# A two-layer retention / convolution / mixture-of-experts trunk: the router's product on two column tiles, slot and block numbers from the position, and its one-hot tables shared out over Pool, ScalarE and VectorE

## The chip, the cores and the metric

One core of one Trainium2 chip runs the whole forward pass. The metric is the device time of one execution in microseconds (us), lower is better. Engines are called as in the profile: PE is TensorE (PEld its weight loads), DVE VectorE, ACT ScalarE, POOL GpSimd, SP SyncE, which here only issues transfers.

## The reference, cut to what matters

512 tokens of width 1024 pass through two layers. Layer 0 mixes tokens by retention, layer 1 by a convolution module; behind each mixer stands a mixture of experts with 4 groups of 8 experts, all in f32. What the change touches is the router ahead of the experts:

```python
    lg = (xt @ w_rg + b_rg).astype(jnp.float32)
    pg = jax.nn.softmax(lg, axis=-1)
    g_idx = jnp.argmax(lg, axis=-1).astype(jnp.int32)
    gate_g = jnp.take_along_axis(pg, g_idx[:, None], axis=-1)
    le = (xt @ w_re + b_re).astype(jnp.float32).reshape(N, MOE_GROUPS, MOE_EXPERTS_PER_GROUP)
    le_sel = jnp.take_along_axis(le, g_idx[:, None, None], axis=1)[:, 0]
    top_v, top_i = lax.top_k(le_sel, MOE_TOPK)
    pe = jax.nn.softmax(top_v, axis=-1)
    wts = (gate_g * pe).reshape(-1)
    eid = (g_idx[:, None] * MOE_EXPERTS_PER_GROUP + top_i.astype(jnp.int32)).reshape(-1)
    ...
        return (jax.nn.silu(xblk @ w_gate[e]) * (xblk @ w_up[e])) @ w_down[e]
    ...
    out = jax.ops.segment_sum(yb * buf_w[:, None].astype(yb.dtype), buf_tok, num_segments=N + 1)[:N]
```

The assignments (two for each token) are sorted by expert and cut into blocks that belong to one expert each; which slot of which block a token lands in is free, as long as its result comes back with its weight.

## The kernel before, in words

**Layers.** In each layer the mixer comes first (weight tiles split in two parts by ACT and POOL, products on PE), then x is turned (transposed) by PE (turn_x, L640), then the router runs (route: PE L712, DVE L1022), then the experts (PE L795, DVE L1136, ACT L496, POOL L445 to L456).

**Experts.** The 1024 assignments are laid out in blocks of 32 rows; each block belongs to one expert, an expert has at least one block, and there are 47 blocks in each layer here (the 94 executions of the lines of a block are two layers of 47). Block by block PE multiplies by gate and up (L770), by down (L790), picks the rows of the next block from the normed x by one-hot products (pick_rows, L700), turns them (L709), and sends the result of the block before to its tokens (put_rows, L753). The weights of an expert are three transfers of 2 MB on SP's queue (L361 to L381); nine places in SBUF hold three experts. The first three experts are loaded ahead of the router or under it; the transfer for expert 3 and every later one waits until the blocks of the expert that holds the place are done (semaphores gu_half, gu_mm, y_mm).

**The router, in the order in which each engine meets it.** The order is written by hand, and each engine runs its own list in order.

- PE: eight products of the turned x with the router's weights (L716), all into the same 36 partitions of bank 0; it waits for DVE's copy of the result, turns it in four pieces (L721) and then runs six matmuls whose result nobody reads (stay_awake, L651). It waits for the one-hot table of experts, counts with nine products (L728, L730), runs four more unread matmuls, picks the rows of block 0 (L700), turns them (L709), waits for spread_ready and multiplies the table of slots with the table of blocks (L742), which gives for each block the token and the weight of each row. Then the first expert begins (L770).
- ACT: copies the even pieces of the turned x (L487), then squares x and takes roots (L467, L468), scales x by the reciprocal root (L493), and takes two exponentials (L498, L500). Then it waits for the first block.
- DVE: copies the odd pieces (L961), then takes the reciprocal of the roots (L966), and only after it copies the product (L1024); then some forty small instructions in a chain (Link.done, L88, waits for each before the next is issued) up to pos (L1090), the row of every assignment among all blocks. know_rows (L988) makes from pos the one-hot rows of block 0. Five small steps (L1093 to L1097) make the slot in the block and the number of the block from rank and base. Then come block_hot (L1100, 576 columns a partition), slot_hot_r (L1103, 1024 columns), the copy of the picked rows (stage, L1020), and three copies of block_hot scaled by the three rows of coef (L1107, L1110, L1112), with turned_block (L1008) in between. After them it makes the rows of block 1 and reads the product L742.
- POOL: has nothing in the router. It waits for idx_ready and for the token numbers (L445, L446), whose transfer SP issues after idx_mm (L358).
- SP: the transfer into place 8 waits for the end of the router's product (L354), the loop over the later experts for cum_ready and idx_mm (L356, L357).

The three scaled tables are written over by the later experts' work; slot_hot_r lies where sine and cosine lay before.

Of the kernel before, what the change touches and what calls it, by code (L numbers as in the profile page):

```python
# [21 lines left out]
ALU = mybir.AluOpType  # L22
ACT = mybir.ActivationFunctionType
# [6 lines left out]
P = 128  # L30
# [27 lines left out]
C_EYE, NCONST = 630, 662  # L58
# [34 lines left out]
def program(nc, x_in, pos_in, const_in, decay_in, par_in, w_qk, w_v, w_g, w_out, w_pw1, w_pw2, b_pw2,  # L93
            w_router, b_router, w_gu0, w_gu1, w_down, g_final, tok_in, out):
    with ExitStack() as ctx:
# [104 lines left out]
        logitsT = area_c[0:NG + NE, route_at:route_at + S]  # L200
# [8 lines left out]
        ranki, blki = room[:, 1816:1824].bitcast(I32), room[:, 1824:1832].bitcast(I32)  # L209
        count, blocks, upto = room[:, 1832:1864].bitcast(I32), room[:, 1864:1896], room[:, 1896:1928]  # L210
# [47 lines left out]
        def both(name):  # L258
            return sems(name, NL)
# [4 lines left out]
        tok_loaded, slot_known, tok_hot, y_split, y_rounded, first_mm, second_mm, added = (  # L264
            both(n) for n in ("tok_loaded", "slot_known", "tok_hot", "y_split", "y_rounded", "first_mm", "second_mm", "added"))
# [154 lines left out]
        def _(pool):  # L420
# [12 lines left out]
            for l in range(NL):  # L433
                if l == 1:
                    for n in range(pw1_tiles + 2 * TILES):
# [8 lines left out]
                        split_lo(ret_tiles + n, n % NWT, n // TILES % 4, tile_column(False, n % TILES))  # L444
                pool.wait_ge(idx_ready[l], 1)  # L445
# [14 lines left out]
        def _(act):  # L460
# [35 lines left out]
            def expert_blocks(l):  # L496
# [3 lines left out]
                nc.scalar.activation(expert_exp, expert_exp, ACT.Exp).then_inc(exp_ready[l], 1)  # L500
                act.wait_ge(cum_ready[l], 1)
# [128 lines left out]
        def _(pe):  # L630
# [81 lines left out]
            def route(l):  # L712

                for k in range(KT):
                    pe.wait_ge(hT_odd if k % 2 else hT_even, 4 * l + k // 2 + 1)
                    last = nc.tensor.matmul(ps[0:NG + NE, 0, :], wr[:, l, k, :], hT[:, k, :],  # L716
                                            start=(k == 0), stop=(k == KT - 1))
                last.then_inc(logitT_mm[l], 1)
                pe.wait_ge(logitT_ready[l], 1)
                for i in range(NT):  # L720
                    last = nc.tensor.transpose(ps[:, 1, i * 64:i * 64 + NG + NE], logitsT[:, i * P:(i + 1) * P],  # L721
                                               ident[0:NG + NE, 0:NG + NE])
# [17 lines left out]
                pe.wait_ge(spread_ready[l], 1)  # L740
                for j in range(8):
# [199 lines left out]
        def _(dve):  # L941
# [80 lines left out]
            def route(l, gain):  # L1022
                dve.wait_ge(logitT_mm[l], 1)
                V.tensor_copy(logitsT, ps[0:NG + NE, 0, :]).then_inc(logitT_ready[l], 1)  # L1024
# [17 lines left out]
                for i in range(NT):  # L1042
# [48 lines left out]
                                       op0=ALU.mult, op1=ALU.add).then_inc(hot_step[l], 1)  # L1091
                know_rows(l, 0)
                link.done(V.tensor_copy(ranki[:, :], rank[:, :]))  # L1093
                link.done(V.tensor_single_scalar(blki[:, :], ranki[:, :], 5, ALU.arith_shift_right))
                link.done(V.tensor_single_scalar(ranki[:, :], ranki[:, :], BLK - 1, ALU.bitwise_and))
                link.done(V.tensor_copy(rank[:, :], ranki[:, :]))
                link.done(V.tensor_tensor(base[:, :], base[:, :], blki[:, :], ALU.add))  # L1097


# [3 lines left out]
                link.sent(V.tensor_tensor(slot_hot_r[:, :, :],  # L1103
                                          const[:, C_MOD:C_MOD + P].unsqueeze(1).to_broadcast([P, 8, P]),
                                          rank[:, :].unsqueeze(2).to_broadcast([P, 8, P]), ALU.is_equal))
                stage(l, 0)
                link.sent(V.tensor_tensor(block_hot_r[:, 0], block_hot[:, :, :],  # L1107
                                          coef[:, 0, :].unsqueeze(2).to_broadcast([P, 8, NBLK]), ALU.mult))
                turned_block(l, 0, gain)
                link.done(V.tensor_tensor(block_hot_r[:, 1], block_hot[:, :, :],  # L1110
                                          coef[:, 1, :].unsqueeze(2).to_broadcast([P, 8, NBLK]), ALU.mult))
                V.tensor_tensor(block_hot_r[:, 2], block_hot[:, :, :],  # L1112
                                coef[:, 2, :].unsqueeze(2).to_broadcast([P, 8, NBLK]), ALU.mult) \
                    .then_inc(spread_ready[l], 1)
                know_rows(l, 1)
# [228 lines left out]
def shape_constants():  # L1344
# [9 lines left out]
    c[:, C_QOFF] = p // BLK - 4  # L1354
# [68 lines left out]
```

## Time and profile before

| | us |
|---|---|
| median of 3 runs | 1647.12 |
| the 3 runs | 1646.97, 1647.12, 1655.14 |
| the profiled execution | 1646.21 |
| its span, first to last instruction | 1644.2 |
| PE busy in the span | 1547.2 (94%) |
| DVE busy | 967.9 (59%) |
| ACT busy | 467.8 (28%) |
| POOL busy | 424.9 (26%) |
| mean granted TensorE clock | 0.986 |

The profiled execution has 2.0 us around its span. Times in a timeline are us from the start of the span; layer 0's router runs from 444 to 473, layer 1's from 1137 to 1166.

### The profile page before, as it was taken

To read this page: it belongs to the slowest core of one execution; us is meant where nothing else is said; L and a number is where in the kernel's file an instruction comes from. 1 tells how busy PE (TensorE), PEld (TensorE's weight loads), DVE (VectorE), ACT (ScalarE), POOL (GpSimd) and SP (SyncE) were. 2 spreads that over 40 slices of the span, in tenths; PEclk is the share of its full clock that TensorE was granted. 3 is DMA by queue.
4 is the path that set the end of the run, shared out by engine and by line. 5 is a ranking of instruction groups with operands and counts; after the bars stand their busy time and mean duration, and the time that the engine had idled before them with its cause. 6 is when DMAs were issued, how large, how long until landed. Compare 5 with 4: busy or idle time off the path is not lost.

```text
span 1644.2 us, 45941 instructions
## 1 busy us (share of the span) xinstructions
PE 1547.2 (94%) x19216; PEld 1008.3 (61%) x19217; DVE 967.9 (59%) x1669; ACT 467.8 (28%) x802; POOL 424.9 (26%) x371
## 2 busy tenths in 40 slices
PE   7999999999989999999889899889899999989996
PEld 6868678687645555555455588556555555555553
DVE  4222112220377777777657889943777777767777
ACT  5242422423312222222212432054122222222223
POOL 3434344243101121121112255511011121111211
PEclk9999999999999999999999999999999999999998
DMA  9212122122479999999999421036199999999994
GB/s 372 102 53 101 53 83 81 67 85 97 159 310 427 428 428 429 429 428 428 428 429 428 209 103 52 23 121 266 44 428 427 428 429 428 428 429 428 430 428 186
DMA packets 33849, 457.57 MB, mean 278 GB/s; under 512 B 3840, under 2 KB 3968, under 8 KB 6400
## 3 DMA queue, kind: packets, MB, share of 16 engines
q1 hardware_dynamic: 33648, 456.55, 66.5%
q8 instruction: 46, 0.75, 0.2%
q10 hardware_dynamic: 144, 0.17, 0.0%
q14 instruction: 11, 0.09, 0.0%
HBM read 454.61 MB, written 2.10 MB: 278 GB/s over the span
## 4 chain that ended last, share of the span: by engine, by line
PE 83%; DMA 8%; DVE 4%; issue 2%; ACT 2%; POOL 1%; DVEq 0%; SPq 0%; ACTq 0%; POOLq 0%
PE ps L770 19%; PE ps L658 10%; PE ps L660 10%; PE ps L659 10%; PE ps L790 9%; PE ps L700 9%; PE ps L753 7%; DMA area_b<-w_gu 6%; DMA ring<-w_down 2%; PE ps L858 2%; PE ps L709 2%; PE ps L782 1%; POOL area_c L439 1%; PE ps L908 1%; PE ps L850 1%
## 5 line engine op out<-in xcount | busy, mean ns | idle before, releaser
L1132 DVE TENSOR_TENSOR x<-x,ps 128x1024 f32<-128x1024 f32 x384 | 458.9, 1216 | 132.3 <-PE ps L753 132.3
L455 POOL TENSOR_SCALAR slot_tok<-trig,slot_now 128x512 fp32r<-128x512 f32 x94 | 147.0, 1564 | 719.3 <-PE ps L753 719.3
L424 POOL TENSOR_TENSOR w_lo<-ring,w_hi 128x512 fp32r<-128x512 f32 x176 | 237.8, 1354 | 356.1 <-ACT w_hi L474 356.0
L770 PE MATMUL ps<-ring,hgT 128*32 128x256 f32 x4160 | 255.9, 387 | 24.8 <-issue 21.0
L474 ACT CAST w_hi<-ring 128x512 fp32r<-128x512 f32 x176 | 108.8, 622 | 345.2 <-PE ps L660 345.2
L770 PEld LDWEIGHTS ps<-ring,hgT 128*32 128x32 f32 x4160 | 127.7, 111 | 122.0 <-issue 41.9
L700 PE MATMUL ps<-area_a,block_rows 128*32 128x256 f32 x3072 | 184.1, 380 | 2.6 <-DVE block_rows L1000 2.6
L700 PEld LDWEIGHTS ps<-area_a,block_rows 128*32 128x32 f32 x3072 | 100.4, 110 | 70.1 <-issue 5.3
L506 ACT ACT_TABLE_LOAD x94 | 120.6, 1283 | 33.2 <-DVEq L1122 31.5
L658 PE MATMUL ps<-w_hi,hT_hi 128*128 128x512 f32 x320 | 125.0, 391 | 2.9 <-DVE hT_lo L1322 2.9
L790 PE MATMUL ps<-ring,aT_e 128*32 128x256 f32 x2080 | 125.7, 382 | 0.2 <-DMA ring<-w_down 0.2
L659 PE MATMUL ps<-w_lo,hT_hi 128*128 128x512 f32 x320 | 124.6, 389 | 0.0
L660 PE MATMUL ps<-w_hi,hT_lo 128*128 128x512 f32 x320 | 124.5, 389 | 0.0
L753 PE MATMUL ps<-y_hi,slot_tok 32*128 32x256 f32 x1536 | 120.8, 329 | 2.8 <-DVE y_lo L1150 2.8
L511 ACT ACTIVATE y_hi<-ps,slots 128x256 fp32r<-128x256 f32 x94 | 44.6, 475 | 261.2 <-PE ps L790 261.2
L753 PEld LDWEIGHTS ps<-y_hi,slot_tok 32*128 32x128 f32 x1536 | 74.4, 184 | 55.3 <-issue 40.1
L506 ACT ACTIVATE sg_e<-ps 128x128 f32<-128x128 f32 x94 | 26.1, 278 | 274.1 <-PE ps L770 274.1
L658 PE MATMUL ps<-hT_hi,w_hi 128*128 128x512 f32 x256 | 99.8, 390 | 3.2 <-DVEq L1171 2.5
L753 PE MATMUL ps<-y_lo,slot_tok 32*128 32x256 f32 x1536 | 100.5, 276 | 0.0
L1020 DVE COPY hg<-ps 128x256 f32<-128x256 f32 x96 | 40.8, 425 | 100.4 <-PE ps L700 100.4
L659 PE MATMUL ps<-hT_lo,w_hi 128*128 128x512 f32 x256 | 99.6, 389 | 0.0
L660 PE MATMUL ps<-hT_hi,w_lo 128*128 128x512 f32 x256 | 99.6, 389 | 0.0
(217 smaller groups left out, 2067.4 us busy)
## 6 DMA issues: line engine op xcount, KB each, us to landing
ring<-w_gu SPq DMA_DIRECT2D x88, 2048.0 KB, 21.0
ring<-w_down SPq DMA_DIRECT2D x44, 2048.0 KB, 22.6
area_c<-w_gu SPq DMA_DIRECT2D x20, 2048.0 KB, 23.4
area_b<-w_gu SPq DMA_DIRECT2D x20, 2048.0 KB, 25.9
hT<-w_down SPq DMA_DIRECT2D x20, 2048.0 KB, 25.9
ring<-w_pw SPq DMA_DIRECT2D x6, 2048.0 KB, 11.1
ring<-w_qk SPq DMA_DIRECT2D x4, 2048.0 KB, 9.5
ring<-w_v SPq DMA_DIRECT2D x4, 2048.0 KB, 8.8
```

The source lines that it names most:

```text
L424: nc.gpsimd.tensor_tensor(w_lo[:, place, :], ring[:, s, at:at + 512], w_hi[:, place, :].bitcast(F32), ALU.subtract).then_inc(lo_ready, 1)
L455: nc.gpsimd.tensor_scalar(slot_tok[:, :], tok_number, slot_now[:, 0:1], None, ALU.is_equal).then_inc(tok_hot[l], 1)
L474: nc.scalar.copy(w_hi[:, place, :], ring[:, s, at:at + 512]).then_inc(hi_ready, 1)
L506: nc.scalar.activation(sg_e[:, :], ps[:, 2, 0:P], ACT.Silu).then_inc(silu_ready[l], 1)
L658: nc.tensor.matmul(at, lhs[0], rhs[0], start=start, stop=False)
L659: nc.tensor.matmul(at, lhs[0], rhs[1], start=False, stop=False)
L660: return nc.tensor.matmul(at, lhs[1], rhs[0], start=False, stop=stop)
L700: last = nc.tensor.matmul(ps[32 * g:32 * g + 32, 0, 0:QW], block_rows[:, i, :], xn[:, i, g * QW:(g + 1) * QW], start=(i == 0), stop=(i == ...
L753: last = nc.tensor.matmul(ps[:, bank + g, i * QW:(i + 1) * QW], slot_tok[rows, cols], part[rows, :], start=(i == 0 and n == 0), stop=(i == ...
L770: last = nc.tensor.matmul(ps[32 * g:32 * g + 32, 2, 0:256], hgT[:, n * (KT // 2) + k, :], gate_up[n][:, k, :, g * P:(g + 1) * P], start=(n ...
L790: last = nc.tensor.matmul(ps[32 * g:32 * g + 32, 3, P:P + QW], aT_e[:, k * BLK:(k + 1) * BLK], down[:, k, g * 256:(g + 1) * 256], start=(k ...
L1132: return V.tensor_tensor(x[:, i, :].rearrange("p (g c) -> p g c", g=4), x[:, i, :].rearrange("p (g c) -> p g c", g=4), ps[:, bank:bank + 4 ...
```

## The change

The product's even k go to column tile 0 (partitions 0 to 35) and its odd k to column tile 64 (partitions 64 to 99); the copy takes all 100 partitions, and the four turns become products with a constant of zeros and ones (C_HALVES) that adds the two halves. pos is cast to an integer ahead of know_rows; slot and block number come from it by a mask and a shift. The table of slots is written by POOL in eight pieces of 128 columns, the second scaled table by ACT in eight pieces of 72 columns; the first scaled table moves ahead of stage. PE waits for both before L742, DVE for ACT's pieces before the third table and for POOL's before know_rows of block 1. The constants' tensor gains 36 columns (NCONST goes from 662 to 698), from column 662 on.

```diff
-        logitsT = area_c[0:NG + NE, route_at:route_at + S]
+        logitsT = area_c[0:64 + NG + NE, route_at:route_at + S]
@@ -442,6 +443,10 @@
+                pool.wait_ge(rank_ready[l], 1)
+                for j in range(8):
+                    nc.gpsimd.tensor_scalar(slot_hot_r[:, j, :], const[:, C_MOD:C_MOD + P], rank[:, j:j + 1], None,
+                                            ALU.is_equal).then_inc(slots_hot[l], 1)
@@ -498,6 +503,10 @@
+                act.wait_ge(blocks_hot[l], 1)
+                for j in range(8):
+                    nc.scalar.activation(block_hot_r[:, 1, j, :], block_hot[:, j, :], ACT.Copy,
+                                         scale=coef[:, 1, j:j + 1]).then_inc(spread_act[l], 1)
@@ -713,13 +722,14 @@
                 for k in range(KT):
                     pe.wait_ge(hT_odd if k % 2 else hT_even, 4 * l + k // 2 + 1)
-                    last = nc.tensor.matmul(ps[0:NG + NE, 0, :], wr[:, l, k, :], hT[:, k, :],
-                                            start=(k == 0), stop=(k == KT - 1))
+                    at = 64 * (k % 2)
+                    last = nc.tensor.matmul(ps[at:at + NG + NE, 0, :], wr[:, l, k, :], hT[:, k, :],
+                                            start=(k < 2), stop=(k >= KT - 2), tile_position=(0, at))
...
-                    last = nc.tensor.transpose(ps[:, 1, i * 64:i * 64 + NG + NE], logitsT[:, i * P:(i + 1) * P],
-                                               ident[0:NG + NE, 0:NG + NE])
+                    last = nc.tensor.matmul(ps[:, 1, i * 64:i * 64 + NG + NE], logitsT[:, i * P:(i + 1) * P],
+                                            const[0:64 + NG + NE, C_HALVES:C_HALVES + NG + NE], start=True, stop=True)
...
                 pe.wait_ge(spread_ready[l], 1)
+                pe.wait_ge(spread_act[l], 8)
+                pe.wait_ge(slots_hot[l], 8)
@@ -1021,7 +1033,7 @@
-                V.tensor_copy(logitsT, ps[0:NG + NE, 0, :]).then_inc(logitT_ready[l], 1)
+                V.tensor_copy(logitsT, ps[0:64 + NG + NE, 0, :]).then_inc(logitT_ready[l], 1)
...
+                dve.wait_ge(hot_step[l], 1)
+                link.done(V.tensor_copy(ranki[:, :], pos[:, :]))
                 know_rows(l, 0)
-                link.done(V.tensor_copy(ranki[:, :], rank[:, :]))
+                link.sent(V.tensor_single_scalar(slot_of[:, :], ranki[:, :], BLK - 1, ALU.bitwise_and))
                 link.done(V.tensor_single_scalar(blki[:, :], ranki[:, :], 5, ALU.arith_shift_right))
-                link.done(V.tensor_single_scalar(ranki[:, :], ranki[:, :], BLK - 1, ALU.bitwise_and))
-                link.done(V.tensor_copy(rank[:, :], ranki[:, :]))
-                link.done(V.tensor_tensor(base[:, :], base[:, :], blki[:, :], ALU.add))
+                V.tensor_copy(rank[:, :], slot_of[:, :]).then_inc(rank_ready[l], 1)
+                link.done(V.tensor_copy(base[:, :], blki[:, :]))
                 link.done(V.tensor_tensor(block_hot[:, :, :],
                                           const[:, C_IOTA:C_IOTA + NBLK].unsqueeze(1).to_broadcast([P, 8, NBLK]),
                                           base[:, :].unsqueeze(2).to_broadcast([P, 8, NBLK]), ALU.is_equal))
-                link.sent(V.tensor_tensor(slot_hot_r[:, :, :],
-                                          const[:, C_MOD:C_MOD + P].unsqueeze(1).to_broadcast([P, 8, P]),
-                                          rank[:, :].unsqueeze(2).to_broadcast([P, 8, P]), ALU.is_equal))
-                stage(l, 0)
+                V.sem_inc(blocks_hot[l], 1)
                 link.sent(V.tensor_tensor(block_hot_r[:, 0], block_hot[:, :, :],
                                           coef[:, 0, :].unsqueeze(2).to_broadcast([P, 8, NBLK]), ALU.mult))
+                stage(l, 0)
                 turned_block(l, 0, gain)
-                link.done(V.tensor_tensor(block_hot_r[:, 1], block_hot[:, :, :],
-                                          coef[:, 1, :].unsqueeze(2).to_broadcast([P, 8, NBLK]), ALU.mult))
+                dve.wait_ge(spread_act[l], 8)
                 V.tensor_tensor(block_hot_r[:, 2], block_hot[:, :, :],
                                 coef[:, 2, :].unsqueeze(2).to_broadcast([P, 8, NBLK]), ALU.mult) \
                     .then_inc(spread_ready[l], 1)
+                dve.wait_ge(slots_hot[l], 8)
                 know_rows(l, 1)
@@ -1352,6 +1361,7 @@
+    c[:, C_HALVES:C_HALVES + NG + NE] = p[:, None] % 64 == np.arange(NG + NE)[None, :]
```

## Rows read from the trace of the kernel before

**Rows 1.** The page: the chain that ended last, by engine; GB/s in 40 slices.
```profile
PE 83%; DMA 8%; DVE 4%; issue 2%; ACT 2%; POOL 1%; DVEq 0%; SPq 0%; ACTq 0%; POOLq 0%
...
GB/s 372 102 53 101 53 83 81 67 85 97 159 310 427 428 428 429 429 428 428 428 429 428 209 103 52 23 121 266 44 428 427 428 429 428 428 429 428 430 428 186
```

**Rows 2.** Timeline, layer 0's product: start, us, engine, line, instructions [idle before <- releaser].
```profile
444.28 7.06 PE L716 MATMUL ps<-hT,wr 128*36 128x512 f32 x16
...
450.04 0.18 DVE L966 RECIPROCAL small<-small 128x4 f32<-128x4 f32 x1 [4.87 <-ACT small L468]
...
451.37 0.68 DVE L1024 COPY area_c<-ps 36x512 f32<-36x512 f32 x1 [1.16 <-PE ps L716]
...
452.11 0.43 PE L721 MATMUL ps<-const,area_c 36*128 36x36 f32 x4 [0.78 <-DVE area_c L1024]
...
452.48 5.42 PE L654 MATMUL ps<-const 128*128 128x512 f32 x12
...
458.98 0.40 PE L728 MATMUL ps<-onehot_r,counting 128*128 128x288 f32 x1 [1.09 <-DVE onehot_r L982]
```

**Rows 3.** Timeline, the same in layer 1.
```profile
1137.13 7.06 PE L716 MATMUL ps<-hT,wr 128*36 128x512 f32 x16
...
1144.17 0.18 DVE L966 RECIPROCAL small<-small 128x4 f32<-128x4 f32 x1 [6.24 <-ACT small L468]
...
1144.26 0.65 DVE L1024 COPY area_c<-ps 36x512 f32<-36x512 f32 x1
```

**Rows 4.** Timeline, layer 0, from the row numbers to the product of the tables.
```profile
464.87 0.16 DVE L1093 CAST area_c<-area_c 128x8 int32<-128x8 f32 x1
...
465.02 1.93 PE L700 MATMUL ps<-area_a,block_rows 128*32 128x256 f32 x32 [1.31 <-DVE block_rows L1000]
...
465.89 0.76 DVE L1100 TENSOR_TENSOR area_c<-const,area_c 128x576 f32<-128x576 f32 x1
466.68 1.22 DVE L1103 TENSOR_TENSOR slot_hot_r<-const,area_c 128x1024 fp32r<-128x1024 f32 x1
467.82 0.42 DVE L1020 COPY hg<-ps 128x256 f32<-128x256 f32 x1
...
469.22 0.75 DVE L1110 TENSOR_TENSOR block_hot_r<-area_c,coef 128x576 fp32r<-128x576 f32 x1
...
470.81 2.04 PE L742 MATMUL ps<-block_hot_r,slot_hot_r 128*128 128x216 f32 x8 [2.08 <-DVE block_hot_r L1112]
```

**Rows 5.** Timelines of POOL and DVE where both work on SBUF.
```profile
25.32 4.43 POOL L424 TENSOR_TENSOR w_lo<-ring,w_hi 128x512 fp32r<-128x512 f32 x3 [4.11 <-ACT w_hi L474]
...
26.93 1.67 DVE L1183 TENSOR_TENSOR area_c<-area_c 128x512 f32<-128x512 f32 x1
...
1044.88 19.95 POOL L439 TENSOR_TENSOR area_c<-area_c 128x512 f32<-128x512 f32 x1 [17.10 <-ACT area_c L607]
...
1047.71 15.99 DVE L1292 SCALAR_TENSOR_TENSOR ring<-area_b,par,ring 128x512 f32<-128x512 f32 x24
```

**Rows 6.** Groups by form: shapes, count | busy us, mean ns | idle before.
```profile
L455 POOL TENSOR_SCALAR slot_tok<-trig,slot_now 128x512 fp32r<-128x512 f32 x94 | 147.0, 1564 | 719.3 <-PE ps L753 719.3
L451 POOL COPY slot_now<-slots 128x1 f32 x94 | 17.4, 185 | 110.2 <-issue 46.2 <-DMA trig<-tok_in 45.2 <-POOL slot_tok L455 18.8
...
L511 ACT ACTIVATE y_hi<-ps,slots 128x256 fp32r<-128x256 f32 x94 | 44.6, 475 | 261.2 <-PE ps L790 261.2
...
L493 ACT ACTIVATE area_a<-x,small 128x1024 f32<-128x1024 f32 x8 | 8.5, 1137 | 0.5 <-DVE small L966 0.5
```

**Rows 7.** Windows: us; busy PE, PEld, DVE, ACT, POOL (count); granted clock, DMA share, GB/s.
```profile
924.00:928.00 4.00, 0.79 (x28) 0.58 (x20) 4.00 (x4) 2.98 (x5) 4.00 (x4) 1.00 0.17 72
928.00:931.00 3.00, 2.47 (x3) 1.18 (x4) 2.96 (x5) 2.94 (x7) 0.66 (x1) 0.50 0.00 0
...
471.00:477.00 6.00, 5.83 (x48) 3.43 (x52) 1.90 (x9) 1.28 (x1) 0.00 (x0) 0.50 0.15 46
```

**Rows 8.** Timeline of POOL, its first tensor_scalar of the run.
```profile
482.40 1.58 POOL L455 TENSOR_SCALAR slot_tok<-trig,slot_now 128x512 fp32r<-128x512 f32 x1 [4.98 <-PE ps L753]
```

More of the change, by code:

```diff
@@ L57 @@
 C_INV, C_QOFF, C_REV4, C_REV32, C_A = 584, 585, 586, 590, 622
-C_EYE, NCONST = 630, 662
+C_EYE, C_HALVES, NCONST = 630, 662, 698
 G_MIX, G_FFN, G_HEAD, B_PW1, B_DW, LN_G, LN_B, W_DW = 0, 16, 32, 48, 64, 72, 80, 88
@@ L209, in program @@
         ranki, blki = room[:, 1816:1824].bitcast(I32), room[:, 1824:1832].bitcast(I32)
+        slot_of = room[:, 1728:1736].bitcast(I32)
         count, blocks, upto = room[:, 1832:1864].bitcast(I32), room[:, 1864:1896], room[:, 1896:1928]
@@ L263, in program @@
         hot_step, rows_known, pick_mm, staged = (both(n) for n in ("hot_step", "rows_known", "pick_mm", "staged"))
-        tok_loaded, slot_known, tok_hot, y_split, y_rounded, first_mm, second_mm, added = (
-            both(n) for n in ("tok_loaded", "slot_known", "tok_hot", "y_split", "y_rounded", "first_mm", "second_mm", "added"))
+        blocks_hot, spread_act, rank_ready, slots_hot, tok_loaded, slot_known, tok_hot, y_split, y_rounded, first_mm, second_mm, added = (
+            both(n) for n in ("blocks_hot", "spread_act", "rank_ready", "slots_hot", "tok_loaded", "slot_known", "tok_hot", "y_split", "y_rounded", "first_mm", "second_mm", "added"))
         gu_half = both("gu_half")
```

## The prediction

> **What bounds the kernel now.** I read the page first: the chain that ended last runs through PE for 83% and DMA for 8%, and the row of GB/s shows both expert stages at 427 to 430 [rows 1]. The experts' weights stream without pause once the first blocks free a place; in layer 1 one slice at 44 GB/s shows that the stream starts only when they do. So the router works by one number per layer, the time at which PE enters the first expert, and what is won or lost there moves the stream and the end with it, one for one. The change touches nothing else. Next I read the timelines of both routers. The reader should see two places. At the product, PE works 7.06 us, but DVE's program has the reciprocal ahead of the copy, and ACT's roots release it at 450.04 in layer 0 and at 1144.17 in layer 1, where the product ends within 0.02 us of it [rows 2, 3]. Before the tables' product, PE has picked and turned its rows and waits for DVE [rows 4].
>
> The sum is made against the profiled execution: 1644.2 of span and 2.0 around it, 1646.21. The median of the runs shown is 1647.12, 0.9 above; one run of 1655.14 stands apart. A measurement of this kernel can tell about 0.5%, 8.2 us, from no change.
>
> **The product.** Sixteen instructions take 7.06 us, 0.44 each, one after the other. pick_rows uses four column tiles already: 32 instructions of 256 columns in 1.93 us [rows 4], 0.06 each, where half of 0.44 would be 0.22 on one tile; tiles do run side by side. Two tiles should give 3.5 us, and PE stands still from 447.8 and from 1140.7. In layer 0 the copy then starts behind the reciprocal, 450.04 + 0.2 = 450.25 instead of 451.37: 1.12 saved of the 3.5. In layer 1 the reciprocal starts at 1144.17 and the copy already at 1144.26: nothing saved. The work that hides the rest is ACT's squares and roots. The copy's duration goes by columns, not partitions, and stays 0.68; the four small products replace four small turns of the same 36 columns at 0.43: nothing. SP's transfer into place 8 is issued 3.5 us earlier, in a queue that is busy anyway or has time: nothing. The larger constants, 5% of a transfer at the start, cost under 0.1 us.
>
> **The clock.** PE now idles from 447.8 to the small products at 451.0 (3.2 us), in layer 1 from 1140.7 to 1145.0 (4.3 us). What such a rest does is in the windows: between 924 and 928 PE works 0.79 of 4 us, and from 928 to 931 the granted clock is 0.50, that is 1.2 instead of 2.4 GHz, while PE works through unread matmuls [rows 7]. I take it to fall in both layers. The small products then cost 0.43 more. The six unread matmuls take 5.42 us from 452.48 and end 1.08 before PE starts to count at 458.98 [rows 2]; a half clock over 3 us of them adds 1.5, of which 0.4 shows. It needn't cover them. I take 0.4 in layer 0 and 0.7 in layer 1, with the longer rest; bounds 0 and 0.9 each.
>
> **Slot and block from pos.** The chain from L1093 to L1100 lasts 1.02 us (464.87 to 465.89) in five steps of 0.2. Now one step stands ahead of know_rows, so that block 0's rows come 0.20 later (PE picks until 467.15), and the table of blocks starts at 465.63, 0.26 earlier. The late pick is covered by DVE's tables until 467.2; without these it would cost its 0.2.
>
> **The tables.** DVE loses slot_hot_r (1.14 from start to start of its neighbours) and one scaled table (0.78). Alone, it would run block_hot 465.63 to 466.39, the first scaled table to 467.17, stage to 467.7, turned_block to 468.7, the third table to 469.45, and PE would start at 469.5, against 470.81 [rows 4]: the lower bound, 1.3 saved.
> ACT's eight pieces: with a scale from memory a row costs 0.475 for 256 columns and 1.137 for 1024 [rows 6], so 0.86 ns a column and 0.32 for 72; eight are 2.5 us, from 466.5 to 469.0, beside DVE's stage and turned_block. Upper bound 8 × 0.475 = 3.8, until 470.3. The third table waits behind it, 0.3 late at most by my value.
> POOL's eight pieces: no row has 128 columns. Between 1.564 for 512 and 0.185 for one [rows 6], a line gives 0.53; a quarter of 1.564 is 0.39. I take 0.50, near the line since an instruction's fixed part is in both rows: 4.0 us, bounds 3.1 and 4.2. From 465.6 on they end at 469.6, were POOL alone.
>
> It isn't. While POOL subtracts from 25.32 on, DVE's tensor_tensor at 26.93 with both operands in SBUF takes 1.67 for 512 columns, where 576 take 0.76 without POOL; and POOL's sum at 1044.88 takes 19.95, with DVE's taps streaming beside it, where three such instructions took 4.43 [rows 4, 5]. block_hot and the first and third scaled tables are all of that kind. Served in turn with POOL's eight, they make one queue: 465.6 + 4.0 + 3 × 0.74 = 471.8, and PE starts at 471.9 at the latest link, 1.0 later than before. That is my value for each layer; the bounds are 1.3 earlier (no conflict, short pieces) and 1.3 later (pieces of 0.53).
> The Trainium skill ("SBUF — State Buffer", the section on two separate sides) calls the pair of ports that GpSimd shares with VectorE an exclusive lock, held for an instruction, and names VectorE instructions with two SBUF inputs. By that rule POOL would be held for one instruction at a time, and the sum is the 471.8 above. The row at 1044.88 is harsher than the rule, since DVE's next instructions went first again and again; by it POOL would begin only at DVE's pause at 467.2, with 467.2 + 4.0 + 0.74 = 471.9. The two hardly differ here.
>
> DVE's new wait for POOL holds know_rows of block 1 (0.9 us), which runs beside L742 (2.04 us): nothing. Behind ACT's new wait stand cum_ready and the first block, 5 us later: nothing. Behind POOL's stand the token numbers, later still: nothing. PE's two new waits hold L742 and the first expert, which is the number above. From 471 to 477 PE runs at 0.50 [rows 7] and I expect the same, since PE again stands still before L742.
>
> **The sum.** Layer 0: -1.1 + 0.4 + 1.0 = +0.3. Layer 1: 0 + 0.7 + 1.0 = +1.7. Together +2.0: 1648.2.
>
> **The rivals.**
> *POOL and DVE don't block each other.* For it: POOL's pieces have one input from SBUF, and neither row of the conflict shows that; the broadcast operands may count otherwise. Against it: rows 5. Then PE starts 1.1 earlier in each layer instead of 1.0 later: 1648.2 - 4.2 = 1644.0. With the shorter wait the clock may stay full where it was 0.50 for 6 us [rows 7], up to 3 us per layer; with one such gain 1641.0, with both 1638.0.
> *The clock costs more than it gives, and the kernel is slower.* The place is the unread matmuls behind the product. The half clock has lasted 6 us once [rows 7]. Over 6 us of them it adds 3.0, minus the 1.08 of slack: 1.9 instead of my 0 to 0.3, in each layer. From about 2.2 us of overlap on it decides. 1648.2 + 3.7 = 1651.9.
> *The first piece on POOL comes late.* POOL's first tensor_scalar in the run, at 482.40, came behind 4.98 us of waiting for PE [rows 8], which could cover a preparation of up to that length. In the new place nothing covers it if it starts with the instruction: POOL would begin at 470.6 and PE at 475.4, 4.6 later than before in layer 0 alone: 1648.2 + 3.6 = 1651.8.
> The Trainium skill ("GPSIMD Engine Reference", instruction dispatch) says that the first call of a freshly loaded POOL routine costs about 6 us more; by that figure 1652.8. No row here shows it, and the 1.58 of that first instruction, against 1.564 for the mean, speaks against a cost within the instruction.
> *The change doesn't do what it says: two tiles with 36 columns don't run side by side.* Then no 1.12 is saved, and no rest arises for the clock: 1646.21 + 2 × 1.0 = 1648.2, the same time by another way.
>
> **How the numbers follow.** Forecast 0.54, no conflict 0.24 (a third of it with a clock that stays full), half clock 0.08, late POOL 0.06, no tiles 0.08. The predicted time is 1648.2. The range must hold the forecast's own bounds (from 1646 to 1650), the two slower rivals with some scatter of the runs (1652.5), and the better part of the first rival (1642.0): 1642.0 to 1652.5. No case alone passes 8.2 us either way; only a clock that stays full in both layers, or two slow rivals together, or a disturbed set of runs does. Faster 0.05, same 0.90, slower 0.05.
>
> **What would show it.** In the trace after: L716's successor takes 3.5 us with its instructions in pairs; the copy starts at about 450.25 in layer 0 and unmoved in layer 1; a window of 0.50 around the unread matmuls; POOL's eight pieces with single ones at 1.2 us instead of 0.5, or DVE's table at 1.2 instead of 0.76; POOL's last piece as what releases L742, at about 471.9. Wrong would be: L742 released by DVE before 470.5, no half clock behind the product, or an end that doesn't follow the first expert's start.

## The result and the profile after

The changed kernel takes 1657.12 us (median of 10 runs, 1653.25 to 1661.56); the kernel before took 1648.34 in 10 runs beside it. The ratio is 1.005, interval 1.0037 to 1.0063: about 8.8 us slower by the medians. I had forecast 1648.2 and a range of 1642.0 to 1652.5. The median is above the range. The difference of the medians is 0.53% of the time before; I had put most of the chance within 0.5%. The direction (slower by 2) was right and the size far too small. Three of the 99 runs of the kernel before that stand beside the experiments took 1783 us and more, in a slow state; they are in no ratio, and without them its three medians below would be 1648.07, 1648.53 and 1647.82.

Layer 0's router after the change, timeline (start, us, engine, line, instructions, and in brackets the idle time before and its releaser):

```profile
445.99 3.63 PE L726 MATMUL ps<-hT,wr 128*36 128x512 f32 x16
...
451.75 0.18 DVE L978 RECIPROCAL small<-small 128x4 f32<-128x4 f32 x1 [4.87 <-ACT small L473]
451.85 0.66 DVE L1036 COPY area_c<-ps 100x512 f32<-100x512 f32 x1
...
452.56 1.92 PE L731 MATMUL ps<-const,area_c 100*128 100x36 f32 x8 [2.94 <-DVE area_c L1036]
...
454.29 7.87 PE L663 MATMUL ps<-const 128*128 128x512 f32 x12
454.52 0.74 DVE L1041 SCALAR_TENSOR_TENSOR area_c<-ps,small,bias_r 128x36 f32<-128x36 f32 x4 [2.02 <-PE ps L731]
...
461.60 0.70 PE L738 MATMUL ps<-onehot_r,counting 128*128 128x288 f32 x1
...
466.51 0.17 DVE L1102 SCALAR_TENSOR_TENSOR pos<-area_c 128x8 f32<-128x8 f32 x1
...
468.20 5.94 POOL L448 TENSOR_SCALAR slot_hot_r<-const,area_c 128x128 fp32r<-128x128 f32 x8 [35.40 <-DVE area_c L1109]
468.21 0.78 DVE L1111 TENSOR_TENSOR area_c<-const,area_c 128x576 f32<-128x576 f32 x1
469.08 2.07 ACT L508 ACTIVATE block_hot_r<-area_c,coef 128x72 fp32r<-128x72 f32 x8 [9.15 <-DVEq L1114]
469.14 0.76 DVE L1115 TENSOR_TENSOR block_hot_r<-area_c,coef 128x576 fp32r<-128x576 f32 x1
...
471.19 0.76 DVE L1120 TENSOR_TENSOR block_hot_r<-area_c,coef 128x576 fp32r<-128x576 f32 x1
...
474.29 2.01 PE L754 MATMUL ps<-block_hot_r,slot_hot_r 128*128 128x216 f32 x8 [3.57 <-POOL slot_hot_r L448]
```

The rows to compare are [rows 2] and [rows 4]. The product is twice as fast (3.63 for 7.06), and the copy waits for the reciprocal, as forecast. Then the reader should see what was not: the turn of the scores is eight instructions in 1.92 us, where it was four in 0.43, and DVE's first score comes 2.67 us after the start of the copy instead of 1.21. The six unread matmuls (L663) take 7.87 instead of 5.42 and now end in the count. At the end the tables' product is released by POOL, not by DVE, which had finished 2.2 us earlier.

In layer 1 the copy gained nothing ([rows 3]: 7.13 us behind the product's start there) and everything else is lost in the same way:

```profile
1145.04 3.63 PE L726 MATMUL ps<-hT,wr 128*36 128x512 f32 x16
...
1152.18 0.66 DVE L1036 COPY area_c<-ps 100x512 f32<-100x512 f32 x1
...
1154.86 0.74 DVE L1041 SCALAR_TENSOR_TENSOR area_c<-ps,small,bias_r 128x36 f32<-128x36 f32 x4 [2.02 <-PE ps L731]
...
1174.31 2.02 PE L754 MATMUL ps<-block_hot_r,slot_hot_r 128*128 128x216 f32 x8 [3.56 <-POOL slot_hot_r L448]
```

I cut every run into the same intervals, each from the start of one instruction to the start of the next named one (us; for PE's count and tables' product the start of their weight load):

| interval | before, layer 0 / 1 | after, layer 0 / 1 |
|---|---|---|
| product to copy | 7.10 / 7.14 | 5.86 / 7.13 |
| copy to first score | 1.21 / 1.18 | 2.68 / 2.68 |
| first score to count | 6.40 / 6.40 | 7.05 / 6.75 |
| count to pos | 4.94 / 4.94 | 4.94 / 4.93 |
| pos to tables' product | 6.88 / 6.89 | 7.75 / 7.74 |
| sum | 26.53 / 26.55 | 28.28 / 29.23 |

The routers lose 1.75 and 2.68, 4.4 us. The profiled executions differ by 12.8 (1646.21 and 1659.01), the medians by 8.8. So half of the loss lies where the change has edited nothing. 1.7 us of the profiled difference stands ahead of layer 0's router: the product starts at 445.99 instead of 444.28, after a stretch at half clock at the very start of the run, before any changed instruction of PE. That is scatter of the executions: in the profiles of all the kernels of this document the product starts between 443.37 and 447.71, and the two ends are e5 and e10, which are the same program up to there. The largest piece lies behind layer 1's layer norm: from its last product to the turn of x 53.98 us instead of 51.29. Windows there, before and then after (us; busy PE, PEld, DVE, ACT, POOL; granted clock, DMA share, GB/s):

```profile
1088.00:1090.00 2.00, 0.18 (x1) 0.21 (x2) 1.07 (x3) 1.94 (x4) 0.00 (x0) 1.00 0.00 0
1090.00:1092.00 2.00, 2.00 (x10) 1.62 (x10) 1.76 (x4) 1.97 (x4) 0.00 (x0) 1.00 0.00 0
```

```profile
1093.30:1095.30 2.00, 0.25 (x1) 0.28 (x2) 1.09 (x2) 1.94 (x4) 0.00 (x0) 0.72 0.00 0
1095.30:1097.30 2.00, 2.00 (x5) 1.54 (x6) 1.76 (x4) 1.97 (x4) 0.00 (x0) 0.50 0.00 0
```

Both kernels have the same rest of 2.9 us for PE. Behind it the one goes on at full clock, ten matmuls in 2 us, the other at half, five.

### The profile page after: what moved, and what is told of

The parts are those of the page before. It is cut to its first block, busy times and chain, and to the rows that moved or that the text cites. A ratio compares the mean times of both kernels' runs of the same rounds, so it can differ in the third digit from the quotient of the medians.

```text
span 1656.4 us, 45903 instructions
## 1 busy us (share of the span) xinstructions
PE 1550.2 (94%) x19224; PEld 1014.6 (61%) x19225; DVE 963.1 (58%) x1665; ACT 472.2 (29%) x818; POOL 435.7 (26%) x387
## 4 chain that ended last, share of the span: by engine, by line
PE 78%; DMA 9%; DVE 8%; ACT 2%; issue 2%; POOL 1%; SPq 0%; DVEq 0%; ACTq 0%
PE ps L782 19%; PE ps L802 9%; PE ps L667 9%; PE ps L709 8%; PE ps L669 8%; PE ps L668 8%; PE ps L765 7%; DMA area_b<-w_gu 6%; DVE area_c L1301 4%; DMA ring<-w_gu 2%; PE ps L870 2%; DVE ring L1301 2%; PE ps L718 2%; PE ps L794 1%; PE ps L663 1%
```

## The experiments

Each was timed in 10 to 12 runs, beside 33 runs of the kernel before on the same chip. The three sets of the kernel before have medians of 1648.33 (beside e1 to e4), 1648.53 (e5 to e8) and 1647.87 (e9 to e12). A difference in us is one of medians. The ratio, which has the interval, isn't their quotient: it puts e2 6.3 us above the kernel before instead of 7.3, e5 4.6 instead of 5.9, and e12 5.8 below instead of 2.5. So differences of 1 us between two times say nothing by themselves. Each kernel has one profile. First I took the change apart.

**e1_product**: the kernel before with the product part alone.

```diff
...
-                    last = nc.tensor.matmul(ps[0:NG + NE, 0, :], wr[:, l, k, :], hT[:, k, :],
-                                            start=(k == 0), stop=(k == KT - 1))
+                    at = 64 * (k % 2)
+                    last = nc.tensor.matmul(ps[at:at + NG + NE, 0, :], wr[:, l, k, :], hT[:, k, :],
+                                            start=(k < 2), stop=(k >= KT - 2), tile_position=(0, at))
...
-                    last = nc.tensor.transpose(ps[:, 1, i * 64:i * 64 + NG + NE], logitsT[:, i * P:(i + 1) * P],
-                                               ident[0:NG + NE, 0:NG + NE])
+                    last = nc.tensor.matmul(ps[:, 1, i * 64:i * 64 + NG + NE], logitsT[:, i * P:(i + 1) * P],
+                                            const[0:64 + NG + NE, C_HALVES:C_HALVES + NG + NE], start=True, stop=True)
```

> The kernel before with the product part alone (two column tiles, turns as products with the constant that adds the halves). Read from the trace after the change: 1.23 us less from the product's start to its copy in layer 0, 0 in layer 1; 1.5 us more from the copy to the first score in each layer; 0.6 and 0.3 us more until pos. Theory 'the sum of the parts': +2.7 us against the kernel before (1651), with a half clock behind the product in both layers. Rival 'the parts work on each other, or the change brings half clocks elsewhere': this part alone gives about as much as the whole, +6 to +9 us (1654 to 1657).

1654.73 us, ratio 1.0039 (1.0024 to 1.0054). Its routers are as expected: copy to first score 2.68 in both layers, first score to count 6.74 and 6.79, the rest as before; together 2.5 us more than before. But the time is 6.4 more. The theory holds for the router; for the time the rival came out (1654 to 1657).

**e2_tables**: the kernel before with the other part alone, that is the changed kernel with the lines above taken back.

```diff
+                pool.wait_ge(rank_ready[l], 1)
+                for j in range(8):
+                    nc.gpsimd.tensor_scalar(slot_hot_r[:, j, :], const[:, C_MOD:C_MOD + P], rank[:, j:j + 1], None,
+                                            ALU.is_equal).then_inc(slots_hot[l], 1)
...
+                pe.wait_ge(spread_act[l], 8)
+                pe.wait_ge(slots_hot[l], 8)
```

> The kernel before with the tables part alone (numbers from pos, POOL's eight pieces, ACT's scaled copy, the new waits). Theory: from pos to the tables' product 7.75 us instead of 6.9, nothing else moves in the router: +1.8 us (1650). POOL's pieces take 0.6 alone and up to 1.2 beside VectorE's tables. Rival 'half clocks elsewhere': +4 us or more. If the first POOL call costs a preparation, layer 0's interval is longer than layer 1's.

1655.64 us, ratio 1.0038 (1.0024 to 1.0051). From pos to the tables' product 7.74 in both layers, as expected, and nothing else in the routers moves: 1.7 us. The time is 7.3 more, so the expected 1650 is missed and the rival (+4 us or more) came out. Layer 0's interval is no longer than layer 1's, so there is no preparation of POOL's on the path.

**e3_turn**: one line, the form of the turn.

```diff
-                    last = nc.tensor.transpose(ps[:, 1, i * 64:i * 64 + NG + NE], logitsT[:, i * P:(i + 1) * P],
-                                               ident[0:NG + NE, 0:NG + NE])
+                    last = nc.tensor.matmul(ps[:, 1, i * 64:i * 64 + NG + NE], logitsT[:, i * P:(i + 1) * P],
+                                            ident[0:NG + NE, 0:NG + NE], start=True, stop=True)
```

> The kernel before with only the turn of the scores changed from four transposes to four plain products with the identity, 36 rows, no column tiles, so no rest ahead of it. Theory 'the form costs': eight instructions instead of four, each with its own weight load; at the full clock about 0.5 us more from the copy to the first score (1.7 instead of 1.2), +1.0 us in all (1649). Rival 'only the half clock makes the turn slow': 1.2 us as before, and no change in time.

1653.91 us, ratio 1.0033 (1.0017 to 1.0049). Its timeline at the turn in layer 0:

```profile
453.49 1.08 PE L721 MATMUL ps<-const,area_c 36*128 36x36 f32 x8 [0.78 <-DVE area_c L1024]
454.61 0.74 DVE L1029 SCALAR_TENSOR_TENSOR area_c<-ps,small,bias_r 128x36 f32<-128x36 f32 x4 [1.17 <-PE ps L721]
```

The form costs: eight instructions, 1.08 us for 0.43 at full clock, and 0.65 on the path in each layer, 1.3 in all. The same eight take 1.92 at half clock in the changed kernel, so of the 1.5 us that the turn lost there, 0.65 are its form and the other 0.84 the clock. Again the time, 5.6 more instead of the expected 1, is 4 above the routers' sum. The twelve runs show more than their median: three take 1648.5 to 1649.6 and nine 1653.6 to 1659.2, with nothing in between. The profiled one is of the three (1649.59). So the extra 4 us comes and goes between executions of one kernel.

**e4_awake**: the changed kernel with PE's rest behind the product filled.

```diff
                 last.then_inc(logitT_mm[l], 1)
+                stay_awake(4, 3)
```

> The changed kernel with three more unread matmuls (2.6 us) behind the product, so that TensorE has no rest there. Theory 'the half clock doubles the turn and delays the count': no half clock there; from the copy to the first score about 1.7 instead of 2.7 us, from there to the count 6.4 instead of 7.05 and 6.75: 3 us less than the changed kernel (1654). Rival 'the form costs all of it, not the clock': the interval stays 2.7 and the time within 1 us of the changed kernel.

1654.19 us, ratio 1.0038 (1.0024 to 1.0052), 2.9 less than the changed kernel. The turn in layer 0:

```profile
447.58 2.84 PE L663 MATMUL ps<-const 128*128 128x512 f32 x6
...
450.59 1.08 PE L732 MATMUL ps<-const,area_c 100*128 100x36 f32 x8 [0.17 <-DVE area_c L1037]
```

With no rest there is no half clock there; copy to first score is 1.83 and 1.84, first score to count 6.41 and 6.40. The routers sum to 2.6 us less than in the changed kernel, and the median follows, though the intervals of the two ratios overlap.

Four kernels, each with an extra of 4 to 6 us that its routers don't hold, though one of them changes a single line by 1.3 us. That pointed away from the change: perhaps any shift of the later stages costs. The next three kernels test that with a delay in layer 0's router, ahead of the third scaled table, made of copies of small tables onto themselves.

**e5_delay17** and **e6_delay34**: the kernel before with a delay (n and m are 3 and 1, or 6 and 2).

```diff
+                if l == 0:
+                    for _ in range(n):
+                        link.done(V.tensor_copy(block_hot[:, :, :], block_hot[:, :, :]))
+                    for _ in range(m):
+                        link.done(V.tensor_copy(coef[:, 2, :], coef[:, 2, :]))
                 V.tensor_tensor(block_hot_r[:, 2], block_hot[:, :, :],
```

> The kernel before with VectorE held up for about 1.7 us in layer 0's router, ahead of its third scaled table, and nothing else. Theory 'a shift of the later stages costs by itself': the four kernels so far lost 4 to 5 us more than their routers did, in rests of TensorE that lie behind the router (start of the convolution layer, behind its layer norm), where the granted clock was at half for longer. Then this one loses 1.7 + 3 to 5 us: 1653 to 1655. Rival 'the extra loss comes from what those changes do in the router': 1.7 us and no more, 1650.

> The same with twice the delay, about 3.4 us. Theory 'the later stages' clock depends on where their rests fall in time, and falls back into place': 3.4 us and little more, 1651 to 1652.5, that is less than the kernel with half the delay. Rival 'every microsecond of delay costs one, and a constant comes on top': 1.7 us more than the kernel with half the delay.

The single delay (1.70 us in the trace) gives 1654.42, ratio 1.0028 (1.0013 to 1.0043): 5.9 us for 1.7 by the medians (by the ratio 4.6, 2.1 to 7.1). The double one (3.39) gives 1651.78, ratio 1.0018 (1.0003 to 1.0033): 3.3 us for 3.4. By the medians twice the delay costs half as much, which no reason inside the router can do. The intervals of the two ratios overlap, but the runs stand apart: eight of the ten with the single delay take 1653.89 or more, ten of the twelve with the double one 1652.52 or less. The interval behind the layer norm is 54.04 us with the single delay and 51.31 with the double one, and 51.29 before. These are one execution each: they show where 2.7 us can be lost, and not how often. The windows of e6 around the rest, at full clock throughout:

```profile
1093.60:1095.60 2.00, 0.46 (x2) 0.45 (x3) 1.29 (x2) 1.94 (x4) 0.00 (x0) 1.00 0.00 0
1095.60:1097.60 2.00, 2.00 (x11) 1.65 (x10) 1.76 (x3) 1.97 (x4) 0.00 (x0) 1.00 0.00 0
```

**e7_after_delay**: the changed kernel with a delay of its own.

```diff
+                if l == 0:
+                    dve.wait_ge(slots_hot[l], 8)
+                    link.done(V.tensor_copy(block_hot[:, :, :], block_hot[:, :, :]))
+                    for _ in range(2):
+                        link.done(V.tensor_copy(coef[:, 2, :], coef[:, 2, :]))
```

> The changed kernel with a delay of about 1.6 us more in layer 0, behind POOL's last piece, so that its layer 0 is about 3.4 us behind the kernel before instead of 1.8. Theory 'the place of the rests decides': the late stages get back what they lost, and the kernel is no slower than the changed one, or 1 to 3 us faster (1654 to 1657). Rival 'a delay is a delay': 1.6 us slower, 1658.7.

1654.07 us, ratio 1.0035 (1.0021 to 1.0049): 3.1 less than the changed kernel, with 1.4 us more from pos to the tables' product in layer 0. By the medians a kernel has become faster by a delay. The intervals of the ratios overlap again; of the runs, nine of the changed kernel's ten take 1655.44 or more and ten of e7's eleven 1655.31 or less. Behind its layer norm stand 51.26 us. The direct test is to fill the rest there.

**e9_after_filled** and **e10_delay17_filled**: the changed kernel, and the one with the single delay, with three more unread matmuls behind the layer norm.

```diff
-            stay_awake(4, 5)
+            stay_awake(4, 8)
```

> The changed kernel with eight instead of five unread matmuls behind the layer norm's last product, so that TensorE's rest of 2.9 us there is filled. Nothing else. Theory 'the later loss is the half clock behind this rest': from the last product of the layer norm to the turn of x 51.3 us as in the kernel before, instead of 54.0, and 2.7 us less than the changed kernel: 1654.4. Rival 'that interval is longer for another reason (the weight tiles, the splits)': 54.0 stays, and no gain.

> The kernel before with the delay of 1.7 us in layer 0 and the same filled rest. Theory: the delayed kernel gets back 2.7 of its 5.9 us: 1651.7. Rival: no gain, 1654.4.

1654.84 (ratio 1.0035, 1.0020 to 1.0051) and 1651.64 (1.0015, 0.9999 to 1.0030): 2.3 and 2.8 less than without the filling. The windows of e9 behind the layer norm, to be set against those of the changed kernel above:

```profile
1091.30:1093.30 2.00, 1.66 (x5) 0.62 (x4) 1.09 (x2) 1.94 (x4) 0.00 (x0) 1.00 0.00 0
1093.30:1095.30 2.00, 2.00 (x10) 1.64 (x10) 1.76 (x4) 1.97 (x4) 0.00 (x0) 1.00 0.00 0
```

and those of e5, the single delay without the filling, to be set against e6's as well:

```profile
1091.30:1093.30 2.00, 0.41 (x1) 0.44 (x2) 1.25 (x2) 1.94 (x4) 0.00 (x0) 0.71 0.00 0
1093.30:1095.30 2.00, 2.00 (x6) 1.52 (x6) 1.76 (x4) 1.97 (x4) 0.00 (x0) 0.50 0.00 0
```

The interval is 51.28 and 51.27 with the filling. The rival fell: the interval isn't longer for another reason. So 2.3 to 2.7 us of the loss outside the routers are this one rest.

**e8_rearranged**: the changed kernel with its parts put where the trace has room.

```diff
                 V.tensor_copy(logitsT, ps[0:64 + NG + NE, 0, :]).then_inc(logitT_ready[l], 1)
+                expert_norm(l, n_norm)
                 dve.wait_ge(logit_mm[l], 1)
...
-                stay_awake(4, 6)
+                stay_awake(4, 8 if l else 6)
...
-                for j in range(8):
+                for j in range(5, 8):
                     nc.gpsimd.tensor_scalar(slot_hot_r[:, j, :], const[:, C_MOD:C_MOD + P], rank[:, j:j + 1], None,
...
                 stage(l, 0)
+                link.sent(V.tensor_tensor(slot_hot_r[:, 0:5, :],
+                                          const[:, C_MOD:C_MOD + P].unsqueeze(1).to_broadcast([P, 5, P]),
+                                          rank[:, 0:5].unsqueeze(2).to_broadcast([P, 5, P]), ALU.is_equal))
                 turned_block(l, 0, gain)
```

(The call of expert_norm ahead of route goes; the waits for POOL ask for 3.)

> The changed kernel rearranged: VectorE copies the product before it takes the reciprocal of the roots, so that TensorE turns it in its rest; eight unread matmuls in layer 1 instead of six; POOL writes three pieces of the slot table and VectorE five, behind its copy of the picked rows. From the rows: from the product's start to the first score 6.0 us in layer 0 and 7.2 in layer 1 (before 8.3 in both), from pos to the tables' product 5.8 (before 6.9): 5.6 us less than the kernel before in the routers, 10 us less than the changed one. Theory: 1641 to 1644; with an unlucky place of the later rests up to 1647. If VectorE's port and POOL's still collide, from pos to the tables' product it is 6.5 or more.

1643.97 us, ratio 0.9970 (0.9959 to 0.9982): 4.6 less than before, 13 less than the changed kernel. Its timeline in layer 0:

```profile
444.54 3.63 PE L726 MATMUL ps<-hT,wr 128*36 128x512 f32 x16
448.22 0.69 DVE L1036 COPY area_c<-ps 100x512 f32<-100x512 f32 x1 [2.78 <-PE ps L726]
448.97 1.08 PE L731 MATMUL ps<-const,area_c 100*128 100x36 f32 x8 [0.79 <-DVE area_c L1036]
...
450.31 0.18 DVE L978 RECIPROCAL small<-small 128x4 f32<-128x4 f32 x1 [1.39 <-ACT small L473]
450.60 0.74 DVE L1042 SCALAR_TENSOR_TENSOR area_c<-ps,small,bias_r 128x36 f32<-128x36 f32 x4
```

The copy comes right behind the product, PE turns the scores at full clock while ACT is still at its roots, and the turn is done before the reciprocal. Product to first score is 6.05 us in layer 0 and 7.33 in layer 1 (8.31 and 8.32 before), pos to the tables' product 5.69 and 5.58 (6.88 and 6.89 before): 5.7 us less than before in the routers, as expected (5.6). The time is at the slow end of what was expected.

**e11_rearranged_filled** and **e12_no_pool**: e8 with the filled rest, and the same without POOL (its loop and the waits for it go as well):

```diff
-                link.sent(V.tensor_tensor(slot_hot_r[:, 0:5, :],
-                                          const[:, C_MOD:C_MOD + P].unsqueeze(1).to_broadcast([P, 5, P]),
-                                          rank[:, 0:5].unsqueeze(2).to_broadcast([P, 5, P]), ALU.is_equal))
+                link.sent(V.tensor_tensor(slot_hot_r[:, :, :],
+                                          const[:, C_MOD:C_MOD + P].unsqueeze(1).to_broadcast([P, 8, P]),
+                                          rank[:, :].unsqueeze(2).to_broadcast([P, 8, P]), ALU.is_equal))
```

> The rearranged kernel with the filled rest. Its profile already shows 51.3 us there, so at most the runs with an unlucky rest gain: 1643 to 1644, the scatter smaller. If three more unread matmuls cost something themselves, it is up to 1 us slower.

> The same with nothing on POOL: VectorE writes all eight pieces of the slot table in one instruction behind its copy of the picked rows; ACT's copy stays. Theory: VectorE's chain is longer by three of eight pieces, from pos to the tables' product 6.1 us instead of 5.6, +1.0 us in all. Rival 'POOL's pieces give nothing since the port holds them': 5.6 as well, and no difference.

e11: 1643.59, ratio 0.9965 (0.9950 to 0.9981), no different from e8, whose profile already had 51.3 us behind the layer norm. The smaller scatter that I expected didn't come: its runs spread over 5.9 us, e8's over 4.3. e12: 1645.36, ratio 0.9965 (0.9946 to 0.9983); pos to the tables' product is 5.97 in both layers instead of 5.69 and 5.57, 0.7 us in all. POOL's three pieces are worth that much; the two times can't tell it, since their intervals cover each other.

## Why the prediction was wrong, step by step

**The product: right.** 3.63 us on two tiles (3.5 forecast), 1.24 saved in layer 0 (1.12), nothing in layer 1.

**The turn of the scores: wrong.** The step that failed reads: "the four small products replace four small turns of the same 36 columns at 0.43: nothing". I had counted columns. The transposes are four instructions in [rows 2] and the products eight in e3, each with a weight load of 128 columns, 0.65 us more on the path at full clock in each layer, 1.3 in all, where the sum had 0. The half clock then took the eight from 1.08 to 1.92. The two together are 1.5 us in each layer, 3.0 in all.

**The clock behind the product: right in kind, too small.** It fell in both layers. The small products lost 0.84 to it in each, not 0.43, as there were more of them, and the count came 0.65 and 0.35 late: 2.7 us in all. The sum had 0.4 and 0.7. The working names two costs, 0.43 for the small products and 0.4 for the unread matmuls, and the sum took only one of them. The rival with the half clock has a slip too: 1.9 in each layer in place of 0.4 and 0.7 gives 1650.9, not 1651.9. Three matmuls (e4) gave 2.6 us in the routers back. So the routers lose 4.4 us instead of 2.0: 1.3 more by the form of the turn, 1.6 more by the clock, and about 0.4 less by the product and the tables.

**The tables: the size was right, the way half.** 0.87 and 0.85 us later, forecast 1.0. But the two engines weren't served in turn. VectorE's tables take 0.78, 0.76 and 0.76 beside POOL, as long as without it, and only POOL waits. POOL's instructions in the changed kernel, by source line (times in ns):

```profile
L448 POOL TENSOR_SCALAR slot_hot_r<-const,area_c x16: 596/598/1192, 468.2 to 1173.6; 128x128 fp32r<-128x128 f32 x16
```

A piece alone takes 0.60 and not 0.50: my line through two rows gave 0.53, nearer, and I had gone below it. The eight of layer 0 take 1.19, 0.99, 0.60, 0.60, 0.92, 0.60, 0.60 and 0.60 in order; the three long ones lie beside VectorE's three tables. In all, the wait is 5.94 - 8 × 0.58 = 1.3 us instead of the 2.2 that I had put down (0.58 is the step from piece to piece), and the pieces are 4.6 instead of 4.0; the errors cancel. The Trainium skill ("SBUF — State Buffer", the section on two separate sides) says that whichever of the two engines starts first gets the pair for its whole instruction and the other blocks. This trace agrees for POOL: each long piece ends 0.40 to 0.47 us after the table that it lay beside. It doesn't for VectorE: its table at 471.19 starts 0.27 us into a piece (470.92, 0.60 long) and still takes 0.76, as alone. My queue had both engines pay.

**ACT: right.** Eight pieces in 2.07 us (2.5), off the path.

**"What is won or lost there moves the stream and the end with it, one for one": wrong, and the larger part of the error.** In layer 0's expert stage it held: from the first expert's first product to its last down product the changed kernel takes 448.85 us, the one before 448.78. In layer 1 the same stretch is 463.82 and was 462.50; No run here gives a reason for these 1.3 us of the profile. It doesn't hold at all for the stages between. Whether the clock falls behind PE's rests in the convolution layer depends on how these rests lie in time, and that depends on what came before and on the execution. By the medians a shift of 1.7 us costs 4 more than itself, one of 3.4 none (e5, e6). The changed kernel's shift in layer 0 is 1.75.

The traces show that this isn't one rest alone. "Start of layer 1" in the table is the time from the last sum of layer 0 to the first product of the convolution, "statistics" that from the layer norm's first product to the first product of its variance (us, one profile of each kernel):

| kernel | at half clock in the start of layer 1 | start of layer 1 | statistics | behind the layer norm |
|---|---|---|---|---|
| before | 1.00 | 95.11 | 7.79 | 51.29 |
| e3 | 2.32 | 95.76 | 8.12 | 51.31 |
| e6 | 2.45 | 95.84 | 8.15 | 51.31 |
| after | 3.22 | 96.24 | 8.33 | 53.98 |
| e5 | 3.58 | 96.37 | 8.44 | 54.04 |
| e4 | 4.15 | 96.67 | 8.58 | 54.09 |

The three go together, also in the kernels that aren't listed: each microsecond at half clock in the start of layer 1 makes it half a microsecond longer, and the ten profiles in which the last rest isn't filled divide cleanly: with up to 2.70 us of half clock at the start the clock stays full behind the layer norm, with 3.22 and more it falls. From the best of these executions to the worst that is 1.6 + 0.8 + 2.8 = 5.2 us without any cost in the routers, which is the size of the extra 4 to 6 us in e1 to e4. And in these stretches the profile of the kernel before is the best of all, and its time is 2.1 us below its own median; of its 96 other runs, 13 take 1654.4 or more, at a mean granted clock of at most 0.983 (the fastest 27, below 1647, have 0.985 or more). So it stands mostly, not always, in a good place.

Of the 8.8 us between the medians, 4.4 are the routers' and 2.3 to 2.7 the rest behind the layer norm (e9). Some 1.7 to 2.1 us are left. The start of layer 1 and the statistics are 1.1 and 0.5 us longer in the changed kernel's profile, each with more half clock in it, and would make 1.7. That the medians differ by just this is not shown; I filled no rest there. The 1.7 us of the profiled difference ahead of the first router can't be the change's.

**The rivals.** "No conflict" fell: POOL's pieces are stretched. "Half clock over the unread matmuls" was partly so: it lasted 6.8 us in each layer, and cost 0.35 to 0.65 at the count. "Late first piece" fell: POOL starts at 468.20 in layer 0, 0.10 after the rank's copy ends, and POOL's configuration instructions for it are at 432.7. By the 6 us of the Trainium skill ("GPSIMD Engine Reference", instruction dispatch) it would have started at 474; no such pause is on the path here. Whether one lies hidden in the 35.40 us in which POOL stood idle before, no run shows. "The tiles don't run side by side" fell. None of my cases held a loss outside the router, and so none reached the 8.8; the range was built from bounds within the router, while the 1655.14 among the three runs of before, 8 us above the others, said that something of that size moved without any edit.

## What to carry to other kernels

Price a change of form by its instructions and not by its columns: an f32 transpose was one instruction here and the plain product of the same shape two, each with its own weight load (e3). If a stage becomes faster but what follows waits for another engine, the gain is a rest for TensorE, and its clock can ask for it back. Look first at what the next instruction in the list of the waiting engine really needs: the faster product gave 1.24 us in one layer and nothing in the other while the copy stood behind the reciprocal, and with the copy ahead of it the first score came another 2.5 us earlier in each layer (e8 beside the changed kernel). The two belong together; before the change the copy of layer 0 waited for the product ([rows 2]), and moving it alone would have given nothing there. And where TensorE has rests of 3 us or so, a change has two costs, its own and that of the shift. Fill such rests before comparing, or run a pure delay of the same size beside the change, and look at the single runs: two groups with a gap say more than their median.

## What the runs showed that I had not expected

- Delay isn't additive: by the medians 1.70 us cost 5.9, 3.39 cost 3.3, and 1.4 more in the changed kernel gained 3.1. The same rest of 2.9 us was followed by the full clock in five profiles (before, e3, e6, e7, e8) and by the half clock in five (after, e1, e2, e4, e5). At half clock it costs 2.7 us of 51.3. This is a matter of the execution and not of the kernel alone: e3's profile has the full clock, and nine of its twelve runs are slower than it by 4.0 us and more.
- POOL yielded to VectorE and not the other way: VectorE's tensor_tensor with two operands in SBUF kept 0.76 to 0.78 beside POOL's tensor_scalar, whose pieces went from 0.60 to 1.19. In [rows 5] it was VectorE that stretched, to 1.67, beside POOL's tensor_tensor with two operands. I haven't separated the form from the order of arrival.
- Two instructions of 36 columns in f32 take 0.27 us at the full clock and 0.48 at half (1.08 and 1.92 for eight): the time nearly doubles with the clock, though so few columns are streamed. That the weight loads set it is my reading, not tested.
